# A one-core retention and mixture-of-experts step: expert weights in pairs of ring slots, rows of 32 KB

## The reference

```python
logits = x @ w_router + b_router
top_val, top_idx = lax.top_k(logits, 4); gates = softmax(top_val)
h = xb @ w_gate_up[e] + b_gate_up[e]            # (rows, 2048)
gate = minimum(h[:, :1024], 7.0); up = clip(h[:, 1024:], -7.0, 7.0)
glu = gate * sigmoid(gate * 1.702)
out = ((up + 1.0) * glu) @ w_down[e] + b_down[e] # (rows, 1024)
y[token] += gate_of_token * out
```

## Time and profile before

| | us |
|---|---|
| median of 3 runs | 1227.98 (1226.54 to 1229.21) |
| the profiled execution, its own time | 1227.6 |
| its span in the trace | 1225.8 |
| PE busy | 1182.8 (96%) |
| DVE, ACT, POOL busy | 296.7, 143.1, 46.2 |
| DMA over the span | 450.85 MB, mean 368 GB/s |

### The profile page before, as it was taken

The page is one execution under the profiler, slowest core; times in us unless marked ns, Lnnn a source line. Parts: engine busy times, 40 slices in busy tenths (PEclk is TensorE's granted clock), DMA queues, the critical chain, the costliest instruction groups (busy, mean ns, idle before and its releaser), DMA issues.

```text
span 1225.8 us, 14701 instructions
## 1 busy us (share of the span) xinstructions
PE 1182.8 (96%) x5911; PEld 623.8 (51%) x5911; DVE 296.7 (24%) x674; ACT 143.1 (12%) x284; POOL 46.2 (4%) x82
## 2 busy tenths in 40 slices
PE   8999999999999999999989999999998999989996
PEld 7888678877443444444343434343443434433432
DVE  4343311223123122121213131313121222212222
ACT  2122111002001101000101010010100000000012
POOL 3032310000000000000000000000000000000000
PEclk9999999999999999999989999999999999999999
DMA  9652775474999999999999999999999999999995
GB/s 323 234 206 97 245 258 208 138 274 167 409 389 422 427 427 428 429 429 428 429 429 430 429 428 428 428 428 427 428 428 428 429 429 428 428 428 428 428 418 217
DMA packets 65902, 450.85 MB, mean 368 GB/s; under 512 B 4449, under 2 KB 35469, under 8 KB 40768
## 3 DMA queue, kind: packets, MB, share of 16 engines
q1 hardware_dynamic: 62432, 438.95, 86.8%
q0 software_dynamic: 3088, 10.77, 2.7%
q10 hardware_dynamic: 344, 0.61, 0.1%
HBM read 444.46 MB, written 6.08 MB: 368 GB/s over the span
## 4 chain that ended last, share of the span: by engine, by line
PE 73%; DMA 24%; DVE 2%; ACT 0%; issue 0%; POOL 0%; DVEq 0%; SPq 0%; POOLq 0%
DMA ring<-in_w_down 24%; PE psum L957 21%; PE psum L968 19%; PE psum L890 19%; PE psum L1040 5%; PE psum L1028 2%; PE psum L1069 1%; PE psum L1070 1%; PE psum L1057 0%; PE psum L756 0%; PE psum L771 0%; PE psum L913 0%; PE psum L958 0%; DVE normed L1832 0%; PE psum L744 0%
## 5 line engine op out<-in xcount | busy, mean ns | idle before, releaser
L957 PE MATMUL psum<-ring,x_T 128*64 128x512 f32 x768 | 350.3, 599 | 0.8 <-DMA ring<-in_w_gate_up 0.4
L958 PE MATMUL psum<-ring,x_T 128*64 128x512 f32 x768 | 350.4, 599 | 0.0
L968 PE MATMUL psum<-ring,act_T 128*64 128x512 f32 x736 | 174.6, 629 | 25.4 <-DMA ring<-in_w_down 25.4
L957 PEld LDWEIGHTS psum<-ring,x_T 128*64 128x64 f32 x768 | 99.4, 137 | 191.1 <-issue 180.6
L890 PE MATMUL psum<-u_T,ring 128*128 128x264 f32 (+1 forms) x576 | 136.2, 391 | 0.0
L1755 DVE TENSOR_TENSOR hg<-psum,params 128x512 f32<-128x512 f32 x32 | 22.1, 692 | 436.7 <-PE psum L1028 436.7
L1040 PEld LDWEIGHTS psum<-one_hot,normed 128*128 128x128 f32 x816 | 101.0, 196 | 39.2 <-issue 38.3
L968 PEld LDWEIGHTS psum<-ring,act_T 128*64 128x64 f32 x736 | 56.7, 144 | 126.2 <-issue 124.7
L890 PEld LDWEIGHTS psum<-u_T,ring 128*128 128x128 f32 x576 | 107.2, 190 | 22.4 <-issue 3.5
L957 PE MATMUL psum<-late_ring,x_T 128*64 128x512 f32 x256 | 118.2, 600 | 0.0
L958 PE MATMUL psum<-late_ring,x_T 128*64 128x512 f32 x256 | 118.2, 600 | 0.0
(11 more groups left out here) (272 smaller groups left out, 871.8 us busy)
## 6 DMA issues: line engine op xcount, KB each, us to landing
ring<-in_w_gate_up SPq DMA_DIRECT2D x96, 2048.0 KB, 27.4
ring<-in_w_down SPq DMA_DIRECT2D x42, 2048.0 KB, 31.4
late_ring<-in_w_gate_up SPq DMA_DIRECT2D x32, 2048.0 KB, 28.8
late_ring<-in_w_down SPq DMA_DIRECT2D x14, 2048.0 KB, 31.5
ring<-in_w_in SPq DMA_DIRECT2D x21, 1024.0 KB, 5.3
ring<-in_w_down SPq DMA_DIRECT2D x12, 1024.0 KB, 26.9
ring<-in_state_ret POOLq DMA_DIRECT2D x8, 512.0 KB, 6.9
out<-ring POOLq DMA_DIRECT2D x8, 512.0 KB, 4.5
```

The lines of the kernel that those rows point to most:

```text
L957: mm(psum[0:CAP, 2 * j + n], x, gate, start=first, stop=final)
L958: last = mm(psum[CAP:P, 2 * j + n], x, up, start=first, stop=final)
L968: last = mm(psum[j * CAP:(j + 1) * CAP, 4 + n], hidden[:, j, 4 * h + i], w, start=h == 0 and i == 0, stop=h == 1 and i == 3)
```

## The change

From body 3 on, chunks are loaded two at a time: one DMA of 4 MB, 32 KB a partition, fills two neighbouring slots and counts on a semaphore of the pair (`pair_in`). For gate-up it brings 4 rows of the matrix a partition; for down it brings a whole matrix, 8 rows a partition. In body 2 only the gate-up chunks come in pairs. `HEAD`, body 1, the down chunks of body 2 and `LAST` keep their 2 MB transfers (and `LAST` its smaller pieces), which now read 16 KB out of each 32 KB. SP issues a pair when the second of its two slots is free. PE waits for a pair at its first chunk. In the down phase of bodies 3 to 14 it waits for both down matrices before half 0, and counts `used` up by 4 after half 1. Bodies 1 and 2 are written out ahead of the loops.

Since the rows have another order, `normed` and `h_raw` are now stored permuted (ACT reads PSUM with a stride and writes blocks), PE's transposes and gathers read consecutive columns, and `turn_hidden` waits for both copies before its first transpose. The biases of gate-up come as 64 rows of 4 KB instead of 128 of 2 KB, turned by 8 transposes instead of 4; the FFN norm's weights are loaded in the same order.

```diff
+BODY1, BODY2 = list(BODY), list(BODY)
...
-        gu_w = ins["w_gate_up"].rearrange("l e (k p i) f -> (l e) p k (i f)", p=P, i=2)
-        dn_w = ins["w_down"].rearrange("l e (k p i) f -> (l e) p k (i f)", p=P, i=4)
+        gu_w = ins["w_gate_up"].rearrange("l e (k p i) f -> (l e) p k (i f)", p=P, i=4)
+        dn_w = ins["w_down"].rearrange("l e (p i) f -> (l e) p (i f)", p=P)
...
+        def as_pair(chunks, c):
+            return chunks is BODY or chunks is BODY2 and chunks[c][1] == "gu"
...
+        def load_pair(sp, chunks, p, c, b):
+            j, part, k = chunks[c]
+            s = chunk_slot(chunks, c, b)
+            if part == "gu":
+                src = gu_w[bass.ds(2 * p + j, 1), :, k // 2, :].rearrange("a p f -> p (a f)")
+            else:
+                src = dn_w[bass.ds(2 * (p - 1) + k // 2, 1)].rearrange("a p f -> p (a f)")
+            sp.dma_start(slots_of_pair(s), src).then_inc(pair_in[s // 2], 16)
...
+                    if as_pair(chunks, c):
+                        if c % 2 == 0:
+                            sp.wait_ge(used, chunk_number(r, chunks, p, c + 1) - RING + 1)
+                            load_pair(sp, chunks, p, c, b)
+                        continue
                     sp.wait_ge(used, chunk_number(r, chunks, p, c) - RING + 1)
                     load_chunk(sp, chunks, p, c, b)
...
+            def stream_bodies(r):
+                stream(r, BODY1, 1, 0)
+                stream(r, BODY2, 2, 1)
+                with sp.Fori(3, NPAIR - 1, 2) as p:
+                    for b in range(2):
+                        stream(r, BODY, p + b, b)
...
-                    for i in range(4):
-                        last = pe.transpose(banks(bank)[:, i * P:(i + 1) * P], rows[:, P + i:5 * P:4], ident)
+                    for i in range(KD):
+                        last = pe.transpose(banks(bank)[:, i * 2 * NE:(i + 1) * 2 * NE], b_rows[:, i:D:KD],
+                                            ident[0:2 * NE, 0:2 * NE])
...
-                    pe.wait_ge(expert_in[s], chunk_there(r, chunks, p, c, b))
+                    if not as_pair(chunks, c):
+                        pe.wait_ge(expert_in[s], chunk_there(r, chunks, c, s))
+                    elif k % 2 == 0:
+                        pe.wait_ge(pair_in[s // 2], pair_there(r, chunks, p, c, b))
...
-                slots = down_there(r, chunks, p, c, b)
                 h = chunks[c][2] // 2
+                if chunks is BODY:
+                    slots = [chunk_slot(chunks, KC + 2 * x + h, b) for x in range(2)]
+                    if h == 0:
+                        for x in range(2):
+                            pe.wait_ge(pair_in[slots[x] // 2], pair_there(r, chunks, p, KC + 2 * x, b))
+                else:
+                    slots = down_there(r, chunks, p, c, b)
...
-                last.then_inc(used, 2)
+                if chunks is not BODY:
+                    last.then_inc(used, 2)
+                elif h == 1:
+                    last.then_inc(used, 4)
...
+                pe.wait_ge(raw_ready, 2 * NE * r + 4 * p + 2 * j + 2)
                 for m in range(KD):
-                    if m % 4 == 0:
-                        pe.wait_ge(raw_ready, 2 * NE * r + 4 * p + 2 * j + 1 + m // 4)
-                    f0 = m // 4 * 4 * P + m % 4
                     last = pe.transpose(psum[:, 6 + m // 4, (m % 4) * P:(m % 4 + 1) * P],
-                                        h_raw[:, j, f0:f0 - m % 4 + 4 * P:4], ident)
+                                        h_raw[:, j, m * P:(m + 1) * P], ident)
...
-                    d0 = k // 2 * 2 * P + k % 2
...
-                                  normed[:, t, d0:d0 - k % 2 + 2 * P:2],
+                                  normed[:, t, k * P:(k + 1) * P],
...
+                body(1, 0, 0, BODY1)
+                body(2, 1, 0, BODY2)
+                bodies(3, BIAS_AT, 0)
...
-                A(normed[0:n, t], banks((4, 6, 0)[t], 2)[0:n], ACT.Copy, scale=rstd[0:n, t:t + 1]).then_inc(xn_ready, 1)
+                A(normed[0:n, t].rearrange("p (k i c) -> p k i c", k=2, i=4),
+                  banks((4, 6, 0)[t], 2)[0:n].rearrange("p (k c i) -> p k i c", k=2, i=4), ACT.Copy,
+                  scale=rstd[0:n, t:t + 1]).then_inc(xn_ready, 1)
...
-                nc.scalar.copy(h_raw[:, j, 0:512], psum[:, 2 * j]).then_inc(raw_ready, 1)
+                nc.scalar.copy(to[:, :, 0:CAP], psum[:, 2 * j].rearrange("p (c i) -> p i c", i=KD)).then_inc(raw_ready, 1)
...
-                nc.scalar.copy(h_raw[:, j, 512:D], psum[:, 2 * j + 1]).then_inc(raw_ready, 1)
+                nc.scalar.copy(to[:, :, CAP:P], psum[:, 2 * j + 1].rearrange("p (c i) -> p i c", i=KD)).then_inc(raw_ready, 1)
```

More of the change, by code:

```diff
@@ L321, in build @@
         rs = msb("rs", 2 * H * DV)
-        rows = rs[:, 0:D]
+        rows, b_rows = rs[:, 0:P], rs[0:2 * NE, P:P + D]
         ret_s = rs.rearrange("p (s h v) -> p s h v", s=2, h=H)
@@ L382, in build @@
         expert_in = [sem(f"expert_in{s}") for s in range(RING)]
+        pair_in = [sem(f"pair_in{q}") for q in range(RING // 2)]
         stored, y_out = sem("stored"), sem("y_out")
@@ L568, in stream @@
                         continue
+                    if as_pair(chunks, c):
[3 more added lines that the diff above has]
+                        continue
                     sp.wait_ge(used, chunk_number(r, chunks, p, c) - RING + 1)
                     load_chunk(sp, chunks, p, c, b)
-            with sp.Fori(1, NPAIR - 1, 2) as p:
-                for b in range(2):
-                    stream(0, BODY, p + b, b)
+            def stream_bodies(r):
[4 more added lines that the diff above has]
+                        stream(r, BODY, p + b, b)
+            stream_bodies(0)
             sp.wait_ge(passes_ready, 1)
@@ L581, in _ @@
                         stream(r, HEAD, None)
-                        with sp.Fori(1, NPAIR - 1, 2) as p:
-                            for b in range(2):
-                                stream(r, BODY, p + b, b)
+                        stream_bodies(r)
                         stream(r, LAST, NPAIR - 1)
@@ L977, in down_there @@
                 for j in range(2):
-                    pe.wait_ge(expert_in[slots[j]], chunk_there(r, chunks, p, c + j, b))
+                    pe.wait_ge(expert_in[slots[j]], chunk_there(r, chunks, c + j, slots[j]))
                 return slots
             def use_down(r, chunks, p, c, b=0):
-                slots = down_there(r, chunks, p, c, b)
                 h = chunks[c][2] // 2
+                if chunks is BODY:
[3 more added lines that the diff above has]
+                            pe.wait_ge(pair_in[slots[x] // 2], pair_there(r, chunks, p, KC + 2 * x, b))
+                else:
+                    slots = down_there(r, chunks, p, c, b)
                 order = [(i, n) for n in range(2) for i in range(4)] if h else [(i, n) for i in range(4)
@@ L1127, in one_pass, with body @@
                         gather(r, 1, c - KC - 1, 0)
+                def body(p, b, added, chunks):
+                    for c in range(KC):
+                        for half in range(2):
+                            use_gate_up(r, chunks, p, c, 0, half, b)
+                        if c == 0:
+                            pe.wait_ge(y_added, ADDS * r + KD * (p - 1 + added) + 1)
+                            turn_hidden(r, p - 1, 1)
+                        else:
+                            gather(r, p + 1, (c - 1) // 2, 2, (c - 1) % 2)
+                    pe.wait_ge(act_ready, NE * r + 2 * p)
+                    use_down(r, chunks, p, KC, b)
+                    turn_hidden(r, p, 0)
+                    gather(r, p + 1, 1, 2, 1)
+                    turn_gated(r, p - 1, 0)
+                    use_down(r, chunks, p, KC + 2, b)
+                    pe.wait_ge(x_ready, 2 * GATHERS * r + 2 * p + 4)
+                    for c in range(2 * KC, 3 * KC):
+                        if c == 2 * KC + 1:
+                            pe.wait_ge(hot_ready, NPAIR * r + p)
+                            pe.wait_ge(out_split, 2 * NPAIR * r + 2 * p + 1)
+                            pe.wait_ge(hidden_took, NE * r + 2 * p + 1)
+                        for half in range(2):
+                            use_gate_up(r, chunks, p, c, 1, half, b)
+                            if 2 * KC + 1 <= c < 2 * KC + 3:
+                                d = 4 * (c - 2 * KC - 1) + 2 * half
+                                scatter(r, p - 1 + added, (d, d + 1))
                 def bodies(first, end, added):
@@ L1132, in bodies @@
                         for b in range(2):
[L1133 to L1146, removed]
-                            turn_gated(r, p - 1, 0)
-                            use_down(r, BODY, p, KC + 2, b)
-                            pe.wait_ge(x_ready, 2 * GATHERS * r + 2 * p + 4)
-                            for c in range(2 * KC, 3 * KC):
-                                if c == 2 * KC + 1:
-                                    pe.wait_ge(hot_ready, NPAIR * r + p)
```

(12 more changed lines are left out.)

44 lines of the change are left out of this document (29 added, 15 removed).

## The result

The changed kernel takes **1259.96 us** (median of 4 runs, 1259.29 to 1261.07) against 1227.26 of the kernel before on the same chip (4 runs, 1226.23 to 1229.21): a ratio of 1.0275, interval 1.0262 to 1.0287 (the two medians alone divide to 1.0267, inside it). It is slower by 33 us; the forecast was 1264, range 1232 to 1277, and slower. Its profiled execution took 1260.59 us with a span of 1258.8.

A forecast was written before the change was run, and what follows sets the result against it. DMA bounds until body 14's down phase, PE after it: start 1102.14 + 9.8 - 6.1 + 31.4 + 1.0 = 1138.2, then 124.0, span 1262.2, 36.4 more; execution 1264 us, range 1232 to 1277.

The forecast's parts named there:

- Longer rows: 32 KB rows in DMA save a fixed 10.2 ns a row, 41 ns a chunk, over 148 chunks: -6.1 us.
- Both down matrices before half 0: Body 14's down phase starts after chunk 4 instead of chunk 2 has landed: 2 x 4.89 = +9.8 us.
- dip: Extra time of a down phase's first half when PE restarts at half clock after longer idle: taken as 2.2 us.
- Slots freed at once: Down slots freed only after half 1, so SP issues the next pair too late and DMA stalls: +31.4 us.
- lead: Time from SP's issue to the landing of the last chunk issued before; 3.9 us needed, or the flow stalls.
- Reads in order: PE's gathers and transposes reading consecutive columns: taken as 0, bound -2 us over PE's own stretches.
- Head +1.0 and tail +0.6: PE waits for ACT's second copy before transposing: +0.6 us in the tail; with larger `normed` copies +1.0 at the head.
- Small stalls: Rival: lead needed is 2.9 or less, or no slow clock; 11 stalls of 0.8 to 1.8 us, 1241 to 1253; chance 0.13.
- No stall: Rival: descriptors arrive in time and only the coarser start remains, 1233 us; chance 0.1.
- the break at 363.5: Trace of the kernel before: chunk issued with lead 1.3 us landed 7.5 after the previous instead of 4.9; held against no stall.
- Faster by rate: Rival: 32 KB rows save more than the fit and no stall comes; 1221 us at three times the fit; chance 0.12.
- Rows split again: Rival: long rows are split into 16 KB in the engines, forecast without the 6.1 us, 1270; chance 0.03.

The follow-up runs named there:

- kernel with halves: Changed kernel, but down matrices of all bodies in 2 MB halves, waited for and freed per half; gate-up stays in 4 MB pairs: 1223.72 us, 0.998 of the kernel before.
- first kernel: Kernel before, with PE waiting for all four down chunks ahead of half 0 in bodies 1 to 14, release unchanged: 1233.67 us, ratio 1.006.
- In the second: Kernel with halves, plus PE waiting for all four down chunks ahead of half 0 in bodies 3 to 14: 1231.44 us, ratio 1.0045.
- two pairs of experiments: Wait for all four down chunks and late release, each alone and both; both on the kernel before: 1276.61 us, both on the kernel with halves: 1262.41 us.
- table of the third question: Lead and stall of bodies 3 to 13 in the changed kernel (1259.96 us) and the kernel with the operations moved (1236.0 us).
- kernel with four added matmuls: Changed kernel with four unread matmuls of 512 columns put ahead of each down phase of bodies 3 to 14: 1251.79 us, ratio 1.0216.
- kernel with the operations moved: Changed kernel with the 23 small PE operations between the down halves (transposes, gather, turns) moved ahead of half 0 in all bodies: 1236.0 us, ratio 1.007.

## Why the prediction was right

**What bounds the kernel, and where.** Right. In the changed kernel no wait for a down chunk comes after 1136.11, and the way from there to the end is 1258.8 - 1136.11 = 122.7 us (124.0 forecast).

**Longer rows, -6.1.** Right. An unstalled pair lands every 9.71 us (9.70 forecast), two single chunks of the kernel before in 9.79: 40 ns a chunk, 41 forecast. For an engine, 8 rows in each, that is 1213 ns a row of 32 KB against 612 for 16 KB, so doubling saves 10 to 11 ns as fitted. The kernel with halves starts body 14 3.9 us earlier (1098.23 against 1102.14), where 100 chunks of 41 ns make 4.1; but 1.5 of it is there in body 1 already, before any pair (353.43 against 354.89), so the even landings are the better proof. By the Trainium skill (DMA: Bandwidth & Descriptors, Why small descriptors are slow) it would have been an estimated 3.5 ns a row; the trace doesn't agree. By the Trainium skill (same page, Where 436 GB/s comes from) the ceiling is 435 GB/s; that agrees with the steady 431 to 434 of the changed kernel (a pair in 9.71 us is 432), though single slices of the kernel with halves read up to 438.

**Both down matrices before half 0, +9.8.** The mechanism is right: alone it cost 7.9 us in one kernel and 7.7 in the other, and the start of body 14 moved by 9.3 and 9.8, counted from body 1. The missing 2 us are in the way from body 14 to the end. In the first kernel it was 1.9 shorter: 1.0 of it is a first half of 8.53 instead of 9.55 us, 0.7 a wait for DVE in the last pair of 0.81 instead of 1.51. In the second the kernel that it is compared with waits 2.17 and 1.20 us in its tail; a later start lets those waits go, and a dip (8.78) takes part of it back. I had counted no such give-back.

**Slots freed at once, +31.4.** Right in place, cause and sum; two details of its working are not. Summed over the landings of pairs, the first pair into the down slots was late by 1.9 us in body 3 (1.8 forecast), by 2.1 to 3.2 in the bodies with a dip (3.0) and by 2.1 in body 9 (2.6): 27.6 us. Another 4.1 us are three delays of 1.2 to 1.5 us at other places (last section). Together 31.7; since the kernel before has one such delay too (0.9 us), 30.8 of it are the change's. The two pairs of experiments give 31.4 and 33.5 for the interaction. So the sum was met partly by luck: the stalls after a dip are smaller than my 3.0, 2.6 in the mean, and a small loss that I did not have fills the place. By the Trainium skill's fixed part of 2.0 us (same page, Anatomy of one DMA) it would have been an estimated 21; the trace doesn't agree, though that page's figure is for another queue.

The first detail that failed is the lead as a hard limit: "the lead needed is 3.9", so that the stall is 3.9 less the lead. The table of the third question shows the scatter: with a lead near 0 the stalls are 2.1 to 3.2; at 2.3 they are 1.9 there and 0.6 to 2.4 in the kernel with four added matmuls; between 3.0 and 4.0 they are anything from nothing to 1.3. Summed over the bodies of the kernel with the operations moved the rule does better (5.5 us for 6.8 measured) than body by body; what else decides stays open. For body 9 the prediction didn't follow its own rule either: it took 2.9 where a lead of 0.3 in a running queue would have 3.9 (2.6 us instead of 3.6; measured 2.1). The second detail is the landing on an empty queue: behind a negative lead the pair came 2.4 to 2.8 us later than its transfer takes from the issue on, not 2.9. The dip itself was well taken: I put it at 2.2, first halves 9.3; measured were 8.88 to 9.88, 9.4 on average, 2.3.

**The beat.** Distances of down phases are 60.2 to 61.5 us (61.2 forecast), but for the three around body 9 with its bias: 64.4, 59.7 and 62.1 (63.0 forecast for the first). Idle 4.7 to 6.5 (4.8 to 5.8), first wait in body 3 (1.8, forecast 1.3), no idle and no dip in body 9: as read from before.

**Reads in order, 0.** A little more than nothing. Operations of the changed kernel:

```profile
L1083 PEld LDWEIGHTS psum<-consts,h_raw x256: 137/140/144, 313.5 to 1212.0; 128*128 128x128 f32 x128
...
L1094 PEld LDWEIGHTS psum<-one_hot,normed x816: 186/192/192, 291.6 to 1189.8; 128*128 128x128 f32 x164
...
L1392 ACT COPY h_raw<-psum x32: 586/586/587, 311.1 to 1208.9; 128x512 f32<-128x512 f32 x32
```

ACT's copy through a stride takes the 586 ns of the plain one; the gather's loads are 192 instead of 196. `turn_hidden` takes 1.09 us instead of 1.23 in a down phase, and between bodies 2 and 3, where nothing is waited for until 463.36, PE's pace is 0.5 us a body better (53.7 against 54.2). In the bodies DMA sets the time, so it only lengthens the idle; in the tail, which is PE's, it may be part of what made it 1.3 us shorter than forecast, but no run isolated that. 0.7 us of the 1.3 are something else: the wait for DVE in the last pair is 0.81 us instead of 1.51, in this kernel as in the one with the wait alone, whose reads are in the old order.

**Head +1.0 and tail +0.6.** The head is the one term with the wrong sign: the first down phase starts at 354.29, 0.6 us earlier than before, within noise of nothing. The tail's wait for the second copy is there, 0.78 us (0.6 forecast):

```profile
1211.30 1.06 PE L1083 MATMUL psum<-consts,h_raw 128*128 128x128 f32 x8 [0.78 <-ACT h_raw L1394]
```

**The sum.** Start of body 14's down phase 1138.2 forecast, 1136.11 measured (head -1.6, stalls and late pairs 30.8 instead of 31.4); tail 1.3 shorter; span 3.4 shorter. With the 0.6 us by which the profiled execution is above the median that is the 4 us between 1264 and 1260.

**The rivals.** Small stalls (1241 to 1253): the dips came in all bodies but 3 and 9, and with them stalls of 2.1 to 3.2 us, not 0.8 to 1.8. No stall (1233): that is about what the wait alone costs, 1231.44 and 1233.67; the break at 363.5 was the right evidence against it. Faster by rate: the rate rose as fitted and no more. Rows split again: they were not.

## What to carry to other kernels

When a ring's slots are freed in larger groups, count from the start of the phase that frees them to the release, and compare it with the transfers still queued at that start: by itself the grouped release cost nothing where the queue was full (and 9 us in the one body where it wasn't), the coarser wait 8 us, and together they cost 31 us more. If such a group must be released late, take everything out of the stretch between its first use and its release that can stand elsewhere; here 3.1 us of small operations moved into a wait gave back 25 us. Enlarge only the transfers that don't sit on this path: gate-up pairs alone kept two thirds of the gain of the longer rows without any of the loss.

## What the runs showed of the hardware that was not expected

- **How late an issue may come has no sharp place in these runs.** In the kernel with the small operations moved ahead nothing was lost at leads of 4.8 us and more, but nothing either in one body at 3.0 and one at 3.7, while at 3.4, 3.6 and 4.0 the stalls were 0.8 to 1.3. In the kernel with four added matmuls, four issues with the same lead of 2.3 us were followed by stalls of 0.6, 1.4, 1.8 and 2.4.
- **A pair can land late in a full queue.** Three pairs of the changed kernel landed 1.2 to 1.5 us late with the queue full. The DMA view of that kernel from 818.7 to 829.5, the first of the three (packets, MB, share of the 16 engines):

```profile
q1 hardware_dynamic: 159, 4.69, 100.8%
q8 instruction: 1, 0.02, 0.6%
```

In each of the three a single fetch of instructions (16 KB) ran beside the pair, and so it did in the longest stall, body 4's 3.2 us. But a fetch isn't enough for it: in the stretches 404.8 to 414.4 and 504 to 513.7 one ran too, and the pairs came in 9.7 us. That the fetch has a part in it was inferred from the coincidence; no run took it away.
- **PE reads consecutive columns faster.** The weight loads of `turn_hidden`'s transposes went from 209 ns (stride 4) to 140, those of the gather (stride 2) only from 196 to 192.
- **The slow restart of PE has no sharp place in this kernel.** In the kernel with four added matmuls it came after idles of 2.56 to 2.94 us, not after 1.24 to 1.76, and not after 3.54 either. In the kernel before it came once after 2.17 and was absent once after 3.02. Nor does its size follow the idle: 6.51 us of idle were followed by a first half of 8.90, 4.69 by one of 9.88.
